# Layers 1 and 2 of a two-block transformer kernel: tile 2's output product, residual, norm and expert input are issued inside tile 3's attention

## What is computed

```python
hl = hl + ml[:, :, 2] * yl
xl = _rmsnorm(hl, norm2_g[i]) * (1.0 + ml[:, :, 4]) + ml[:, :, 3]
hl = hl + ml[:, :, 5] * _peer_ffn(xl, pr_w_q[i], pr_keys[i], pr_u[i], pr_v[i])
```

```python
u = jnp.take(u_tab, ix, axis=0)
a = jax.nn.gelu(jnp.einsum('ted,td->te', u, hx), approximate=False)
vv = jnp.take(v_tab, ix, axis=0)
return jnp.einsum('te,ted->td', gx * a, vv)
```

## Time and profile before

| | us |
|---|---|
| median of 3 runs (4275.89 to 4282.33) | 4279.31 |
| the profiled execution | 4273.91 |
| its span on the core | 4272.1 |
| PE busy (85% of the span) | 3628.6 |
| DVE busy (64%) | 2735.6 |
| ACT busy (38%) | 1633.3 |
| POOL busy (33%) | 1423.2 |

### The profile page before, as it was taken

One profiled execution on the slowest core, in us unless ns is written; L12 is line 12 of the kernel. 1 busy time (PEld: TensorE's weight loads), 2 busy tenths in 40 slices (PEclk: granted clock), 3 DMA queues, 4 the chain that ended last, 5 costly groups with the idle time before them and its releaser, 6 DMA issues.

```text
span 4272.1 us, 42472 instructions
## 1 busy us (share of the span) xinstructions
PE 3628.6 (85%) x11838; PEld 1709.2 (40%) x11838; DVE 2735.6 (64%) x6857; ACT 1633.3 (38%) x4893; POOL 1423.2 (33%) x1319
## 2 busy tenths in 40 slices
PE   7988988888888898898888988988888887888886
PEld 3444433334334343354333433544333334433332
DVE  2246766767777677457676775377666756767675
ACT  1033344444444444242444442224434431444443
POOL 0000434444444444203443442024434421444442
PEclk9989999999999999999999999999999999999999
DMA  5454999999999999866999999569999986999998
GB/s 216 153 197 164 365 422 421 422 420 414 417 418 415 416 411 411 340 252 282 421 421 421 420 412 369 230 243 422 421 421 420 412 354 248 410 422 421 421 414 334
DMA packets 204558, 1560.53 MB, mean 365 GB/s; under 512 B 22752, under 2 KB 22752, under 8 KB 27936
## 3 DMA queue, kind: packets, MB, share of 16 engines
q0 software_dynamic: 189360, 1361.14, 77.1%
q1 hardware_dynamic: 14832, 196.54, 11.8%
q10 hardware_dynamic: 128, 0.13, 0.0%
HBM read 1556.54 MB, written 1.18 MB: 365 GB/s over the span
## 4 chain that ended last, share of the span: by engine, by line
DMA 47%; PE 26%; DVE 9%; ACT 5%; issue 3%; DVEq 1%; POOL 1%; ACTq 0%; POOLq 0%; SPq 0%
DMA arena<-uv,idx 46%; PE banks L1025 14%; PE banks L566 4%; DVE arena L2213 4%; PE banks L695 2%; ACT diag L1369 1%; DMA weight_ring<-weights 1%; PE banks L599 1%; ACT wgt L1367 1%; POOL arena L513 1%; ACT gel L1365 1%; ACT L1365 1%; ACT L1141 1%; PE banks L1052 1%; PE banks L580 1%
## 5 line engine op out<-in xcount | busy, mean ns | idle before, releaser
L1025 PE MATMUL banks<-arena,diag 128*128 128x512 f32 x5120 | 2496.5, 624 | 512.9 <-ACT diag L1369 508.2
L513 POOL DMA_INDIRECT arena<-uv,idx x1280 | 1403.3, 1096 | 2173.0 <-PE banks L1025 1769.4
L2213 DVE CUSTOM_DVE_ANT_0 arena<-arena 128x1024 f32<-128x1024 f32 x1280 | 1566.8, 1224 | 865.8 <-DMA arena<-uv,idx 856.2
L1025 PEld LDWEIGHTS banks<-arena,diag 128*128 128x128 f32 x5120 | 925.6, 195 | 1916.5 <-ACT diag L1369 1140.2
L1365 ACT ACTIVATE gel<-dot 128x1 f32<-128x1 f32 x1280 | 258.6, 202 | 1625.1 <-DVE dot L2213 1623.8
L1369 ACT ACTIVATE diag<-consts_sb,wgt 128x128 f32<-128x128 f32 x1280 | 513.9, 402 | 93.8 <-issue 7.3
L1367 ACT ACTIVATE wgt<-gel,gate 128x1 f32<-128x1 f32 x1280 | 376.9, 294 | 89.9 <-issue 2.5
L566 PE MATMUL banks<-weight_ring,arena 128*128 128x512 f32 (+2 forms) x812 | 349.3, 589 | 13.0 <-DMA weight_ring<-weights 7.7
L566 PEld LDWEIGHTS banks<-weight_ring,arena 128*128 128x128 f32 x812 | 153.6, 191 | 201.9 <-issue 181.6
L695 PEld LDWEIGHTS banks<-arena,weight_ring 128*128 128x128 f32 x1408 | 170.3, 192 | 39.7 <-issue 39.0
L695 PE MATMUL banks<-arena,weight_ring 128*128 128x128 f32 x1408 | 170.7, 275 | 0.0
(11 more groups left out here) (286 smaller groups left out, 2275.7 us busy)
## 6 DMA issues: line engine op xcount, KB each, us to landing
weight_ring<-weights SPq DMA_DIRECT2D x65, 2048.0 KB, 8.2
arena<-weights SPq DMA_DIRECT2D x20, 2048.0 KB, 12.3
arena<-uv,idx POOLq DMA_INDIRECT x1280, 15.2
row_ring<-mods POOLq DMA_DIRECT2D x20, 512.0 KB, 11.7
row_ring<-gains POOLq DMA_DIRECT2D x14, 512.0 KB, 14.2
arena<-keys SPq DMA_DIRECT2D x4, 1024.0 KB, 13.5
weight_ring<-weights SPq DMA_DIRECT2D x2, 1536.0 KB, 10.4
arena<-weights SPq DMA_DIRECT2D x3, 1024.0 KB, 10.1
```

The costliest lines, as they stand in the source:

```text
L513: pool.indirect_dma_start(out=ring[:, RING_SLOT[k], :], out_offset=None, in_=A[f"uv{l}"], in_offset=bass.IndirectOffsetOnAxis(ap=idx[:, UN ...
L1025: ins = mm_(bank[:, yb, :], diag[:, s, :], ring[:, s, D + hf * 512:D + hf * 512 + 512], start=first, stop=last, skip_group_check=True)
L2213: sig(V.tensor_tensor_reduce(out=ring[:, s, 0:D], in0=ring[:, s, 0:D], in1=xnat_of(u[0], u[1]), scale=1.0, scalar=0.0, op0=ALU.mult, op1=A ...
```

## The change

In layer 1, tile 2's `tile_out` goes into the loop: the transposes at the end of step 20, `out0` of step 22, `out1` of step 24, and tile 2's expert input is transposed at the end of step 32. DVE does the residuals in steps 23 and 25 and the norm's pieces in steps 26 to 30. In layer 2 the transposes stand in step 12, `out0` in step 13, `out1` in step 15; DVE does the residuals in steps 14 and 16, the statistics in step 17, the root in step 18, and the rest after the loop; the transposes of the expert input stay behind the loop. Behind the loop PE transposes tile 3's output, does the first two queries, and then tile 3's two products. The modulation blocks stand in earlier steps. Buffers move: the transposed mixer outputs to the second ring slot, so that the eighth gather, not the seventh, waits for tile 3's `out1`, and one buffer of layer 2 by 1024 columns.

```diff
--- before.py
+++ after.py
@@ -106,13 +106,13 @@
 RAW, QKT, VML, OSIG = 4096, 6160, 8208, 10272
 DQT, DKT, DV, MIX = 13344, 15392, 17440, 19488
 L1_MIX = 14592
-MIX_T_OF = {0: {0: 13312, 1: 14336, 2: 9216, 3: 10240}, 1: {2: 9216, 3: 10240}, 2: {2: 9216, 3: 10240}}
+MIX_T_OF = {0: {0: 13312, 1: 14336, 2: 9216, 3: 10240}, 1: {2: 11264, 3: 12288}, 2: {2: 11264, 3: 12288}}
 ATS, EW0, DMASK, MROW = 23584, 25632, 27680, 28192
 EW1 = RAW
 GW = ATS
 L1_QN, L1_KN, L1_QT, L1_KT, L1_V, L1_P, L1_PT = 4096, 6144, 18688, 9216, 10240, 16640, 17664
 L2_Z, L2_CQT, L2_CKVT, L2_KRT, L2_QNT, L2_QR, L2_QRT, L2_KNT, L2_V = (
-    4096, 6912, 7680, 8704, 9216, 11264, 4096, 13312, 17408)
+    4096, 6912, 7680, 8704, 9216, 11264, 5120, 13312, 17408)
 L2_MIX, L2_P, L2_PT = 21504, 23552, 24576
 L3_Z, L3_POOLT, L3_YT = 17408, 19456, 9216
 RESID = XNAT + 2 * D
@@ -271,8 +271,8 @@
 
 
 MODS_L0 = (1, 3, 5, 7, 9, 11, 13)
-MODS_L1 = (0, 2, 5, 8, 11, 14, 17, 20)
-MODS_L2 = (0, 1, 3, 5, 7, 9, 11)
+MODS_L1 = (0, 2, 4, 6, 9, 11, 14, 16)
+MODS_L2 = (0, 1, 2, 4, 6, 8, 10)
 
 
 class Steps:
@@ -508,7 +508,7 @@
                         k = slot_at(u, j)
                         if RING_BEFORE[k] is not None:
                             pool.wait_ge(*after("sum", RING_BEFORE[k]))
-                        elif RING_SLOT[k] == 0:
+                        elif RING_SLOT[k] == (1 if l in (1, 2) else 0):
                             pool.wait_ge(*after("mm", l, "out1", 3, 0))
                         pool.indirect_dma_start(
                             out=ring[:, RING_SLOT[k], :], out_offset=None, in_=A[f"uv{l}"],
@@ -862,6 +862,16 @@
                                 vk = H[:, kk, 256:512] if kk < 2 else v1[:, kk, :]
                                 ins = mm_(bank[:, b, 0:64], prT[:, kk, :], vk[:, kvh * 64:kvh * 64 + 64], start=kk == 0, stop=kk == 3)
                             ins.then_inc(sems["pe"], done("pe", ("mm", 1, "O", i)))
+                        if step == 20:
+                            first = tile_out(2)
+                            next(first)
+                        if step == 22:
+                            next(first)
+                        if step == 24:
+                            next(first)
+                        if step == 32:
+                            for _ in peer_input(r0, LAT[:1]):
+                                pass
                     assert next(beside, 0) == 0
                 if l == 2:
                     natural(2, "zq", LAT[:1], xs, KC, 384, last=False)
@@ -937,6 +947,11 @@
                             for kk in range(4):
                                 ins = mm_(bank[:, b, 0:P], prT[:, kk, :], v2[:, kk, h * P:(h + 1) * P], start=kk == 0, stop=kk == 3)
                             ins.then_inc(sems["pe"], done("pe", ("mm", 2, "O", i)))
+                        if step == 12:
+                            first = tile_out(2)
+                            next(first)
+                        if step in (13, 15):
+                            next(first)
                     assert next(beside, 0) == 0
                 out_tiles = MIX_TILES[l]
                 if l == 0:
@@ -988,16 +1003,15 @@
                         pass
                     for j in range(2):
                         natural(0, f"out{j}", LAT, ms, KC, 512)
-                if l in (1, 2):
-                    first, second = tile_out(2), tile_out(3)
-                    next(first)
+                if l == 1:
+                    second = tile_out(3)
                     next(second)
-                    for _ in first:
+                    for _ in chain(query(units[0]), query(units[1]), second):
                         pass
+                if l == 2:
+                    second = tile_out(3)
                     next(second)
-                    for _ in lead(2):
-                        pass
-                    for _ in second:
+                    for _ in chain(lead(2), second):
                         pass
                 if l == 3:
                     for t in LAT:
@@ -1300,6 +1314,10 @@
                             i = step - 2
                             b = b_(1, "PT", i)
                             ev(a.copy(v(L1_PT + (i % 2) * 512, 512), bank[:, b, :]), 1, "PT", i)
+                        if step == 21:
+                            copy_T((1, "mT"), 2, mT_of(1, 2)[:, 0:4, :], 0)
+                        if step == 33:
+                            next(first)
                 if l == 2:
                     for c in range(8):
                         if c % 2 == 0:
@@ -1333,6 +1351,8 @@
                             i = step - 2
                             b = b_(2, "PT", i)
                             ev(a.copy(v(L2_PT + (i % 2) * 512, 512), bank[:, b, :]), 2, "PT", i)
+                        if step == 12:
+                            copy_T((2, "mT"), 2, mT_of(2, 2)[:, 0:4, :], 0)
                 if l == 3:
                     act.wait_ge(*after("sum", slot_at(units_of(2)[-1], TOPK - 1)))
                     for t in LAT:
@@ -1350,8 +1370,7 @@
                     for t in MIX_TILES[0]:
                         copy_T((0, "mT"), t, mT_of(0, t)[:, 0:4, :], 0)
                 if l in (1, 2):
-                    for t in LAT:
-                        copy_T((l, "mT"), t, mT_of(l, t)[:, 0:4, :], 0)
+                    copy_T((l, "mT"), 3, mT_of(l, 3)[:, 0:4, :], 0)
                 for _ in first:
                     pass
 
@@ -2022,6 +2041,13 @@
                                 ins = V.tensor_tensor(x, x, l1_sink(g).unsqueeze(2).broadcast_to([P, 8, 64]), ALU.mult)
                                 if g % 2:
                                     sig(ins, ("mix", 1, 2 + t))
+                        if step == 20:
+                            copy_T((1, "mT"), 2, mT_of(1, 2)[:, 4:8, :], 1)
+                        if step == 23 or 25 <= step <= 30:
+                            dve.drain()
+                            next(late)
+                        if step == 32:
+                            run(peer_input(r0, (ta,)))
                 if l == 2:
                     z = v3(L2_Z, 4, 704)
                     nm, mg = row(2, "mlag", 0)
@@ -2095,8 +2121,13 @@
                         if step in (10, 18):
                             dve.drain()
                             sig(dve.drain(), ("mix", 2, 2 if step == 10 else 3))
+                        if step == 12:
+                            copy_T((2, "mT"), 2, mT_of(2, 2)[:, 4:8, :], 1)
                         if 11 <= step < 15:
                             next(folded)
+                        if step in (14, 16, 17, 18):
+                            dve.drain()
+                            next(late)
                 if l == 3:
                     for t in LAT:
                         if t == 3:
@@ -2114,14 +2145,14 @@
                 if l == 0:
                     for t in MIX_TILES[0]:
                         copy_T((0, "mT"), t, mT_of(0, t)[:, 4:8, :], 1)
-                if l in (1, 2):
-                    for t in LAT:
-                        copy_T((l, "mT"), t, mT_of(l, t)[:, 4:8, :], 1)
+                if l == 1:
+                    copy_T((1, "mT"), 3, mT_of(1, 3)[:, 4:8, :], 1)
                 run(late)
-                run(peer_input(r0, (ta,)))
+                if l == 2:
+                    copy_T((2, "mT"), 3, mT_of(2, 3)[:, 4:8, :], 1)
+                if l != 1:
+                    run(peer_input(r0, (ta,)))
                 after_topk = mixer_residual((tb,))
-                if l in (1, 2):
-                    next(after_topk)
                 if l in (0, 3):
                     run(after_topk)
                 if l == 0:
```

## The result

The changed kernel takes 4296.41 us (median of 8 runs, 4290.62 to 4299.22), the kernel before 4279.31 (8 runs beside it): ratio 1.0037, 95% interval 1.0027 to 1.0048, so 17.1 us or 0.37% slower. The prediction was 4289.7: direction right, 6.7 us too little. The profiled execution took 4297.51 us (span 4295.7).

The account below looks back on a forecast made before the run. Full DMA engines bound the expert rounds, the chain to the first gather the mixers between. Layer 1 -1.5, layer 2 +1.9 and the blocks +10.0 sum to +10.4 us, so 4289.7; range 4277 to 4297 for 8 in 10.

Parts of the forecast that it names:

- The block: Rounds of layers 1 and 2: second query block (2.10 MB) moves beside the gathers, 5.0 us a layer, 10.0 for both.
- Layer 1's attention: Tile 3's attention grows by 23.3 us against 24.8 removed behind it, so the first query comes 1.5 us earlier.
- step 20's scores to step 22's: Layer 1's attention: step 22's scores wait for the previous pair's exponentials, 7.9 us instead of 3.9, +3.9.
- step 22's scores to the end of O 22: Layer 1's attention: PE alone sets the length, 21.1 us where it took 9.0, +12.2.
- end of O 22 to the end of O 31: Layer 1's attention: DVE sets the length with residuals and norm, 24.0 us instead of 16.8, +7.2.
- Layer 2: Step 13 to the first query takes 40.7 us instead of 38.7, so the first query comes 1.9 us later.
- From there PE alone runs: Layer 1's attention from step 22's scores: PE's work adds up to 21.1 us, old waits absorbed, +12.2.
- layer 2's upper bound: Layer 2's first query up to 2.5 us later still, since PE stands idle longer ahead of the queries.
- The block costs nothing: Start of a round: DVE sets the pace and the block fits under it; +0.4 us, 4279.7, chance 0.10.
- Interleaving pays: Attention: norm pieces slip between maxima; layer 1 gains 11.8 us, layer 2 2.6; 4274.9 in all, chance 0.14.
- It does not do what it says: Attention: out0 or out1 is not loaded when step 22 or 13 asks; +18 us, 4298, chance 0.05.
- The edits costed at nothing: Third query's 2.5 us wait, a later residual, eighth gather's wait and earlier modulation blocks stay covered; otherwise 1.5 to 3 us.

Follow-up runs that it names:

- after: The changed kernel itself, as profiled, against the kernel before: 4296.41 us, ratio 1.0037.
- b_hold: Kernel before with one added wait: layers 1 and 2's second query block is issued only when the first index list is there; 4286.70 us, ratio 1.0020.
- a_late_q1: Changed kernel with the second query of layers 1 and 2 put between tile 3's two output products; 4289.77 us, ratio 1.0024.
- a_fill: Changed kernel with 22 extra products, results thrown away, where PE waits in layers 1 and 2; 4287.71 us, ratio 1.0017.
- first profile: The original profiled execution of the unchanged kernel before; 4273.91 us, layer 1's mixer 200.12 us.
- l2_only: The change in layer 2 alone, layer 1 as in the kernel before; 4286.45 us, ratio 1.0017.
- second profile: The kernel before, unchanged, profiled once more; 4281.10 us, ratio 1.0004, layer 1's mixer 204.42 us.
- b_mods: Kernel before with the modulation blocks of layers 1 and 2 in the changed kernel's earlier steps, nothing else; 4281.18 us, ratio 1.0004.
- l1_only: The change in layer 1 alone, layer 2 as in the kernel before; 4285.71 us, ratio 1.0016.
- b_again: The kernel before, unchanged, run and profiled a second time; 4281.10 us, ratio 1.0004.
- a_mods: Changed kernel with layer 1's modulation blocks back in the steps of the kernel before; 4294.78 us, ratio 1.0038.

## Why the prediction was right, and where it was too small

**The block: right.** 5.0 us a layer predicted; 4.94 and 4.79 in after, 4.27 and 3.86 in b_hold, 3.3 and 2.4 won back in a_late_q1 by 4.4 us of earlier issue. The four prices lie within the bounds 3.0 to 5.6. The issue within 1 us of the first gather, the mechanism that was hardest to see in the diff, came as written.

**Layer 1's attention: mechanism right, size off, by the clock.** The sum took PE's durations from rows at a granted clock of 1.00 and kept them for a stretch in which the same sum put new waits. Its own terms, from PE's timeline:

| us | predicted | after | a_fill (clock 1.00) |
|---|---|---|---|
| step 20's scores to step 22's | 7.9 | 7.4 | 7.4 |
| step 22's scores to the end of O 22 | 21.1 | 25.4 | 22.0 |
| end of O 22 to the end of O 31 | 24.0 | 26.2 | 23.9 |
| all three | 53.0 | 58.9 | 53.2 |

At the full clock the three terms are right within 0.9 us; the 5.9 us of the miss are the two falls. Against the first profile the first query also comes 1.6 us later by what lies before step 20: 0.8 of it is the wait for the layer's first weights (3.58 instead of 2.81 us). All of it is within the scatter there: from the last gather to step 20's scores, seven profiles of kernels that are before's up to this point take 124.7 to 128.5 us; after takes 129.3, 2.75 of them the modulation block that now lies ahead.

**Layer 2: the same.** From step 12's transposes to the first query 40.7 was predicted; after shows 43.6, a_fill 41.0. `out0` starts at 4.92 (4.9 predicted), `out1` at 19.8 (19.4). What is missing is `out1` (8.80 instead of 7.0) and the transposes of the expert input (1.97 instead of 1.1). Another 1.5 us lie ahead of these steps, where after has two falls and before one; l2_only, with one, has a mixer shorter by 1.2. That too is within the scatter ahead of step 12 (153.4 to 156.6 us in kernels that are the same there).

**The sum.** Against the second profile the mixers were missed by 3.2 and 3.8 us, the blocks by -0.3: 6.7, the whole miss. That this comes out so exactly is in part luck, since the mixers' first parts scatter by 3 to 4 us. A surer account starts behind them: from step 20's scores in layer 1 (in the kernels that do before's modulation block there, less its 2.75 us) and from step 12's scores of L919 in layer 2, to the layer's first gather. Before's program takes 75.3 us in layer 1 in all five profiles that have the fall. Two lines of b_mods show it for layer 1, from 1892.62 to 1967.89:

```profile
1892.62 1.13 PE L842 MATMUL banks<-arena 64*128 64x512 f32 x4
...
1967.89 0.97 POOL L513 DMA_INDIRECT arena<-uv,idx  x1 [44.82 <-DVE gate L2206]
```

| us to the first gather | before's program, clock 1.00 | the same, with its fall | after | a_fill (clock 1.00) |
|---|---|---|---|---|
| layer 1 | 72.5 (before) | 75.3 (b_mods) | 76.9 | 71.2 |
| layer 2 | 56.8 (l1_only) | 59.6 (b_again) | 63.7 | 59.2 |

At the full clock the rearrangement itself gives -1.3 and +2.3 (-1.5 and +1.9 predicted). The falls cost after 5.7 and 4.5 us, but before 2.8 and 2.8, so the clock adds 2.9 and 1.7 to the change. (The four kernels with this layer 1 and no extra products take 74.6 to 76.9, those with this layer 2 63.4 to 63.7.) With the rounds' 9.7 that is 15.3 us of the 17.1 measured (interval 11.6 to 20.5); the rest can't be told from the scatter ahead.

The step that failed is the price of PE's work: "From there PE alone runs" and the sums of layer 2 add durations from rows at a clock of 1.00, so PE's speed was taken as a constant behind waits that the same sums put in. The sign stood in the prediction's own rows: layer 2's first query, seen there as 18 records in 3.71 us, takes 5.44 us as a whole, at a clock of 0.50 from 2812.2 to 2815.6:

```profile
2811.71 5.44 PE L695 MATMUL banks<-arena 128*128 128x128 f32 x32 [0.83 <-ACT arena L1098]
```

It was allowed for in layer 2's upper bound alone. The same program shows a first query in layer 1 of 3.81 us in one profile and 5.73 in the other. The Trainium skill, "TensorE: Matmul & The Clock Gate", section "Part 1: The HAM clock gate", says that the full clock has to be kept up by activity and that the same kernel can differ from run to run in it. These two profiles agree.

**The rivals.** *The block costs nothing*: fallen, by b_hold. *Interleaving pays*: fallen, also at the full clock, since a_fill takes 53.2 us where the rival needed some 10 less. The rule of the Trainium skill, "Perfetto Trace Analysis", section Optimization Strategy, does not come true here, where both regimes are PE's. *It does not do what it says*: fallen; `out0` and `out1` wait for ACT and for DVE, not for a landing. The edits costed at nothing held: the third query waits 2.4 us for its block (2.5 predicted), beside full DMA engines. A rival was missing: that the waits which the change makes would slow the work behind them (layer 2's upper bound had 2.5 us for it, the forecast and layer 1 nothing).

**The range** of 4277 to 4297 held 4296.41 with 0.6 us to spare, and the sum's own upper end, +17.1, is what was measured. That was luck in part: layer 1's bounds held no slower clock.

## What to carry to other kernels

When a change makes PE wait on the critical path, price the work behind the wait at both clocks, and look in the windows view at the granted clock of that stretch, in more than one profile. When a product is moved, follow the weight slot that it frees: a transfer that leaves an idle stretch for a full one costs its bytes, here 4 to 5 us for 2.1 MB. And a wait on PE that can't be removed may be filled with useless products; here 22 of them took 8.7 us off the changed kernel.

## What the runs showed that I had not expected

- The clock fell behind single waits of 1.8 to 2.4 us with PE busy before: in a_mods after 8.00 and 7.22 of 8 us, in b_again after 20 us without a pause and a wait of 2.15. In before's attention PE was down to 2.77 of 4 us twice (1896 to 1900 and 1908 to 1912) at a clock of 1.00. What decides between these was not tried further.
- Two profiles of one program differ by 4.3 us in one mixer (200.12 and 204.42), a quarter of the change's effect, 1.5 us of it ahead of step 20 and the rest from the fall; the rounds agree within 0.1 us (652.98 and 652.96; 658.19 and 658.09).
- In layer 1 a block's price is paid in full by the fourth gather's landing (4.31 us in b_hold) and stays to the last (4.29).
